# Token-major products that step through their weight row by turns between its two halves

## What is computed

```python
h = rms_norm(x, pre_g)
proj = h @ w_in                       # 2048 x 13312
...
vn = layer_norm(v, ...)               # v is a part of proj: a_v
k, v = mem_n @ w_k, mem_n @ w_v
branch = jnp.einsum('bsnc,ncd->bsnd', ys, w_branch)      # 3 x (1024 x 2048)
gates = jax.nn.sigmoid(gate_logits)   # gate_logits is a part of proj, 3 x 2048 wide
merged = jnp.sum(gates * branch, axis=2)
out = merged @ w_out
x = x + rms_norm(out, post_g)
...
h = h + conformer_conv(hn, ...)       # 2048 x 4096, conv, 2048 x 2048
h = h + jnp.square(jax.nn.relu(hn @ w_up)) @ w_down      # 2048 x 8192, 8192 x 2048
return rms_norm_2(h, final_norm_g)
```

## Time and profile before

| | us |
|---|---|
| median of 3 runs | 1995.88 (1995.85 to 1995.94) |
| the profiled execution, its own time | 1996.44 |
| its span in the trace | 1994.4 |
| PE busy | 1979.2 (99%) |
| PEld busy | 1703.0 (85%) |
| DVE busy | 1499.2 (75%) |
| ACT busy | 967.0 (48%) |
| POOL busy | 417.8 (21%) |
| DMA queue of the weights | 375.10 MB, 61.7% of 16 engines |

### The profile page before, as it was taken

The page is one execution under the profiler, slowest core; times in us unless marked ns, Lnnn a source line. Parts: engine busy times, 40 slices in busy tenths (PEclk is TensorE's granted clock), DMA queues, the critical chain, the costliest instruction groups (busy, mean ns, idle before and its releaser), DMA issues.

```text
span 1994.4 us, 28447 instructions
## 1 busy us (share of the span) xinstructions
PE 1979.2 (99%) x11210; PEld 1703.0 (85%) x11210; DVE 1499.2 (75%) x2243; ACT 967.0 (48%) x1346; POOL 417.8 (21%) x310
## 2 busy tenths in 40 slices
PE   9999999999999999999999999999999999999998
PEld 8888888888888788888899988888888888888886
DVE  7867888777799976668899996776567557656755
ACT  6555444434444345547643475554444434434443
POOL 0000234333366630000486743000000000000000
PEclk9999999999999999999999999999999999999999
DMA  9765665555665566666566656666666666666664
GB/s 327 230 181 180 186 189 172 160 159 169 181 187 182 179 190 187 192 213 190 158 175 208 191 172 183 188 198 191 191 191 189 193 195 189 192 193 190 190 192 147
DMA packets 105973, 377.45 MB, mean 189 GB/s; under 512 B 11888, under 2 KB 14448, under 8 KB 105712
## 3 DMA queue, kind: packets, MB, share of 16 engines
q1 hardware_dynamic: 105552, 375.10, 61.7%
q10 hardware_dynamic: 288, 0.53, 0.1%
HBM read 372.90 MB, written 2.69 MB: 188 GB/s over the span
## 4 chain that ended last, share of the span: by engine, by line
PE 82%; DVE 13%; ACT 2%; issue 2%; DMA 1%; DVEq 0%; SPq 0%; ACTq 0%
PE bank L2005 23%; PE bank L2016 12%; PE bank L2071 7%; PE bank L2072 7%; PE bank L2070 7%; DVE wl L1132 5%; PE bank L2053 4%; PE bank L2055 4%; PE bank L2054 4%; PE bank L2087 3%; PE bank L2088 3%; PE bank L2089 3%; ACT wh L730 1%; PE bank L2271 1%; DMA raw<-in_w_bxg 1%
## 5 line engine op out<-in xcount | busy, mean ns | idle before, releaser
L1132 DVE TENSOR_TENSOR wl<-raw,wh 128x1024 fp32r<-128x1024 f32 x608 | 759.5, 1254 | 375.9 <-ACT wh L730 374.3
L730 ACT ACTIVATE wh<-raw 128x1024 fp32r<-128x1024 f32 x680 | 714.1, 1057 | 627.7 <-PE bank L2072 226.3
L2005 PE MATMUL bank<-Hr,wh 128*128 128x512 f32 x1536 | 370.6, 392 | 0.2 <-DVE scrB L1181 0.2
L2005 PEld LDWEIGHTS bank<-Hr,wh 128*128 128x128 f32 x1536 | 281.5, 188 | 55.2 <-issue 0.7
L661 POOL TENSOR_TENSOR wl<-raw,wh 128x1024 fp32r<-128x1024 f32 x72 | 174.3, 2430 | 314.0 <-DVE small L1707 245.8
L2070 PE MATMUL bank<-wh,Yr 128*128 128x512 f32 x560 | 217.9, 389 | 0.0
L2071 PE MATMUL bank<-wl,Yr 128*128 128x512 f32 x560 | 217.8, 389 | 0.0
L2072 PE MATMUL bank<-wh,Yr 128*128 128x512 f32 x560 | 217.8, 389 | 0.0
L2016 PEld LDWEIGHTS bank<-Hr,wl 128*128 128x128 f32 x1536 | 197.4, 191 | 8.8 <-issue 1.1
L2005 PE MATMUL bank<-Yr,wh 128*128 128x512 f32 x832 | 201.6, 392 | 0.3 <-DVE gate_b L1202 0.3
L2016 PE MATMUL bank<-Hr,wl 128*128 128x256 f32 x1536 | 200.6, 283 | 0.0
(11 more groups left out here) (381 smaller groups left out, 2778.1 us busy)
## 6 DMA issues: line engine op xcount, KB each, us to landing
raw<-in_w_up SPq DMA_DIRECT2D x128, 512.0 KB, 3.6
raw<-in_w_dn SPq DMA_DIRECT2D x128, 512.0 KB, 3.5
raw<-in_w_g SPq DMA_DIRECT2D x96, 512.0 KB, 3.6
raw<-in_w_p SPq DMA_DIRECT2D x80, 512.0 KB, 3.7
raw<-in_w_b SPq DMA_DIRECT2D x48, 512.0 KB, 3.6
raw<-in_w_out SPq DMA_DIRECT2D x32, 512.0 KB, 3.6
raw<-in_w_q SPq DMA_DIRECT2D x16, 512.0 KB, 4.1
raw<-in_w_av SPq DMA_DIRECT2D x16, 512.0 KB, 3.6
```

What stands on the lines that cost most here:

```text
L730: e.activation(wh[:, c % WN, :], raw[:, c % RAW, :], ACT.Copy).then_inc(s_hi, 1)
L1132: e.tensor_tensor(wl[:, c % RAW, :], raw[:, c % RAW, :], wh[:, c % WN, :].bitcast(F32), ALU.subtract).then_inc(s_low_v, 1)
L2005: ins = e.matmul(dst, wh[:, s, kk * 128:kk * 128 + 128], pair.both[:, :, k, :], start=i == 0 and kk == 0, stop=i == j.nch - 1 and kk == 7, ...
```

## The change

The kernel's `rh` and `rl` get the same 512 columns in another order of addresses. `woven` takes a row of 512 as two halves of 256 and makes of it a pattern with two steps: the inner one goes from a place in the first half to the same place in the second (1 KB on), the outer one to the next place. So the columns stream as 0, 256, 1, 257, 2, 258 and so on. `tilesM` on the host puts output column 2n at place n of the first half and column 2n+1 at place n of the second, so that the columns reach PE in the same order as before, and the outputs land in the same places of PSUM.

```diff
+        def woven(row):
+
+            return row.rearrange("p (s n) -> p n s", s=2)
...
-                        rh = wh[:, s, kk * 512:kk * 512 + 512]
-                        rl = wl[:, r, kk * 512:kk * 512 + 512]
+                        rh = woven(wh[:, s, kk * 512:kk * 512 + 512])
+                        rl = woven(wl[:, r, kk * 512:kk * 512 + 512])
...
     def tilesM(w):
         k, n = w.shape
-        return np.ascontiguousarray(w.reshape(k // 256, 2, 128, n // 512, 512).transpose(3, 0, 2, 1, 4)
+        return np.ascontiguousarray(w.reshape(k // 256, 2, 128, n // 512, 256, 2).transpose(3, 0, 2, 1, 5, 4)
                                     .reshape(n // 512, k // 256, 128, 1024))
```

## The result

The changed kernel takes 1963.86 us (median of 4 runs, 1963.77 to 1964.09) beside 1995.87 for the kernel before: a ratio of 0.984, 95% interval 0.9823 to 0.9857. It is faster by 1.6%, 32 us, where I had forecast 763 us slower. The profiled execution has a span of 1962.1 us, 32.3 less than before.

The account below looks back on a forecast made before the run. PE was taken as the limit in all stages but the last; 3648 kind M matmuls at 0.2092 us more each add 763 us to the span's 1994.4, giving 2759 us for the median, range 1990 to 2800.

Parts of the forecast that it names:

- What bounds the kernel: PE bounds every stage, so pace changes in its 3648 kind M matmuls enter the total one for one.
- The pace and its parts: Kind M matmuls take 0.2266 us each: 0.2133 for 512 columns at one cycle, 0.0133 not columns.
- The step that failed: Each of kind M's 3648 woven matmuls costs 0.2092 us more at two cycles a column, 763 us in all.
- the premise: PE gets groups of neighbours per access; without successive neighbours each column needs an access, at ACT's rate of 0.83 ns.
- L2316's price of 0.4317: Plain f32 product's pace in us, taken for two cycles a column: 0.2051 us more per woven matmul, 748 us.
- L2005's 1.5 ns: Kind W's single 16 KB jump, 0.2281 against 0.2266 us; at that price for 511 jumps, 2800 us more.
- rival "faster": In kind M, alternating places 1 KB apart avoids a collision, shrinking the 0.0133 us: up to 49 us less, 1947; chance 0.04.
- rival "the jumps are free": PE's pace in kind M stays 0.2266 us, perhaps by keeping two streams apart: 1996 us; chance 0.18.
- The rule of the notes: Memory lines of 16 bytes need two hits; woven columns in kind M have one, half the rate, 778 us more.
- that branch: In kind M a line once read serves its four later hits, so the two-hit requirement is met: sum zero.
- The range: Whole kernel between 1990 and 2800 us, leaving out the dearer and faster cases, chance 0.15 together.

Follow-up runs that it names:

- d2: Changed kernel, one dn job's weight columns streamed in steps of 2 places (0, 2, 4 ... then 1, 3 ...): 452 ns a matmul.
- m2: Changed kernel, one dn job's weight columns streamed as separated neighbour pairs (0, 1, 4, 5, 8, 9 ...): 452 ns a matmul.
- q4: Changed kernel, one dn job's weight columns alternating between the row's halves in steps of 4 (0, 256, 4, 260 ...): 452 ns a matmul.
- d8: Changed kernel, one dn job's weight columns streamed in steps of 8 places: 431 ns a matmul.
- r2: Changed kernel, kind W's moving activations and PSUM target walked by turns in runs of two columns: 328 ns for 512 columns, 166 for 256.
- r1: Changed kernel, stage up's moving activations alone walked as single columns by turns: 216 ns for 512 columns, 112 for 256.
- w4: Changed kernel, one dn job's weight columns alternating between two neighbouring blocks of 4 columns: 216 ns a matmul.
- q2: Changed kernel, one dn job's weight columns alternating between the row's halves in steps of 2 (0, 256, 2, 258 ...): 227 ns a matmul.
- r4 to r32: Changed kernel, weight columns taken by turns from the row's halves in runs of 4, 8, 16 or 32: 250, 243, 240, 236 ns a matmul.

## Why the prediction was wrong, point by point

**What bounds the kernel** was right but for one place: the windows of the earlier trace rows were taken from stages where DVE has room, and from them I wrote that a faster PE would find 13% left. In the scan's stretch DVE had 99.86 of 100 us, a window that the prediction left out. It cost 8 of the 40 us. The page of the kernel before had the sign too, in its shares of the chain that ended last, by engine:

```profile
PE 82%; DVE 13%; ACT 2%; issue 2%; DMA 1%; DVEq 0%; SPq 0%; ACTq 0%
```

13% of that chain on DVE is a reason to look for a stage that DVE bounds, even though PE is busy 99% of the span.

**The pace and its parts** were right: 0.2266 us, of which 0.2133 are columns. That an order of addresses can't make the columns faster holds; every order tried is at one cycle a column or slower.

**The step that failed** is the term of 0.2092 us more for each matmul, 763 us in all, from the premise that a stream in which no two successive columns are neighbours needs one access a column and falls to two cycles. The woven matmul measured 0.2156 us, 0.011 less than before instead of 0.209 more. The premise compared a column with the one just before it; the orders show that the one two before it counts. PE falls to 0.43 to 0.46 us a matmul when a column never shares a piece of four with its second predecessor and the stream does not come back to the piece soon (d2, m2, q4), and in the change it shares it three times out of four. L2316's price of 0.4317 was a good price for the wrong case: d8 has 431.

**L2005's 1.5 ns** were no price of a jump; the median step of its matmuls is 227 ns like L2070's, and the mean is higher by some longer ones. With 256 jumps more (r2) a matmul of kind W costs 0.4 ns for each, and with 512 (r1) less than nothing.

**The rival "faster"** had the right place, size and bound, but not the reason (two places 1 KB apart that avoid a collision: w4's are 16 bytes apart and gain as much). The picture nearest to what was found, two streams that the reader keeps apart, stood under the rival "the jumps are free", with the wrong size. The rival "faster" said that the 0.0133 us beside the columns shrink and gave 1947 if all goes. 0.011 went, and with DVE's share kept back it is 1964. I gave it 0.04 for the reason that plain f32 has only 0.005 on top, "so this rest goes with the rate, not with the neighbourhood". That read one row as if it excluded what it didn't vary. q2 shows what goes with what: same rate, same count of jumps as the change, and the 0.0133 are back when each reader takes two columns of a piece instead of four. Why that is a fixed cost of a matmul stays open.

**The rule of the notes**: the section "Memory Cachelines" of the Trainium skill's "Advanced Engine Details and Errata" asks for at least two hits on a line of 16 bytes. Read for one stream it is contradicted twice, by the change (no successive hits, faster) and by d2 and m2 (two successive hits, half the rate). Read for each of two readers it parts the cheap orders from those at half the rate, though not the 9 to 23 ns of r4 to r32, and the sum by it would have been that no time is lost. Where its sentence and these runs differ, the runs decide. I had written that branch down ("the sum zero") without giving it more than 0.18.

**The range** reached from 1990 to 2800 and missed by 26 us, below the case "free" at its lower end. It left out the "faster" case because of its small chance.

## What to carry to other kernels

A moving operand of type fp32r, the only one tried, costs PE one cycle a column, or up to a tenth more, as long as the columns 1, 3, 5, ... come from a piece of four neighbours at least two in a row, and 2, 4, 6, ... too; where both take all four in a row, in every matmul of a stage, each matmul loses 11 of its 13 ns of overhead, 5% of a matmul of 512 columns, and 8 ns, 7%, of one of 256. The cheapest way there is a layout in which even and odd columns lie apart, made by the host for weights and by stepped writes for activations; plain steps of 2 to 64 places cost double and should not be streamed. Before a gain on the busiest engine is added up over all stages, look for the stage where the next engine has no idle time left.

## What the runs showed of the hardware that I had not expected

- The stream behaves as with two readers: 216 ns (four columns of a piece each), 227 (two; 236 to 250 in runs of 4 to 32), 431 to 461 (one), and 268 to 340 if a reader changes between two pieces and comes back, 487 if between four.
- The gain of a woven matmul is lost again if its neighbours are plain: three products with one woven take 680 ns like three plain ones.
- The overhead of a plain matmul is fixed, 13.3 ns at 256, 320, 384 and 512 columns, and doesn't fall with fewer columns of weights to load (232 ns with 32).
- Runs of 4 to 32 columns by turns between two places cost 9 to 23 ns more than plain, runs of 64 nothing.
- A DVE instruction that starts during a remainder of 2.5 us on POOL was held until POOL had ended, 2.0 to 2.2 us, 14 times in the kernel with sixteen of them in the scan's stretch.
- Patterns that alternate between two places cost DVE 0.8 ns an element more (511 to 714 ns for 256, one operand read and the result written so) and ACT 0.95 (510 to 752 ns, only the result).
